# Attention softmax in a two-layer DiT kernel: the multiplication by the reciprocal sum moves from VectorE to GpSimd

## What is computed

```python
def _attend(q, k, v):
    s = jnp.einsum('bqhgd,bkhd->bhgqk', q * HEAD_DIM ** -0.5, k).astype(jnp.float32)
    p = jax.nn.softmax(s, axis=-1).astype(v.dtype)
    return jnp.einsum('bhgqk,bkhd->bqhgd', p, v)
```

## Time and profile before

| | us |
|---|---|
| Median of 3 runs | 3375.95 |
| Profiled execution, its time | 3370.39 |
| Profiled execution, its span in the trace | 3368.6 |
| Pairs of layer 0 (24 pairs), from 1106.90 to 1200.40 | 93.50 |
| Pairs of layer 1 (16 pairs), from 2898.60 to 2959.90 | 61.30 |
| PE busy over the span | 3188.0 |
| DVE busy over the span | 1731.9 |
| ACT busy over the span | 1409.3 |

### The profile page before, as it was taken

The page is one execution under the profiler, slowest core; times in us unless marked ns, Lnnn a source line. Parts: engine busy times, 40 slices in busy tenths (PEclk is TensorE's granted clock), DMA queues, the critical chain, the costliest instruction groups (busy, mean ns, idle before and its releaser), DMA issues.

```text
span 3368.6 us, 51444 instructions
## 1 busy us (share of the span) xinstructions
PE 3188.0 (95%) x18766; PEld 2650.5 (79%) x18766; DVE 1731.9 (51%) x3150; ACT 1409.3 (42%) x2197; POOL 131.5 (4%) x126
## 2 busy tenths in 40 slices
PE   4999999999989899999999999999899998899898
PEld 2777768888868578877788868787788888699898
DVE  2333357777743833434333343333678775756555
ACT  3222255565534632224322242223655654653544
POOL 0000001010100000000000000000000000000000
PEclk7999999999999999999999999999899999999999
DMA  6534431111122033222432243444211113144454
GB/s 234 175 127 151 153 113 45 50 50 44 54 66 88 14 115 130 99 87 95 168 100 94 94 144 137 162 133 153 73 48 51 61 45 115 60 142 164 152 183 146
DMA packets 101116, 363.43 MB, mean 108 GB/s; under 512 B 11136, under 2 KB 12672, under 8 KB 100864
## 3 DMA queue, kind: packets, MB, share of 16 engines
q1 hardware_dynamic: 98240, 353.02, 31.0%
q10 hardware_dynamic: 2752, 8.72, 0.8%
HBM read 360.58 MB, written 1.11 MB: 107 GB/s over the span
## 4 chain that ended last, share of the span: by engine, by line
PE 84%; DVE 7%; ACT 4%; issue 3%; DMA 1%; POOL 0%; SPq 0%; DVEq 0%; POOLq 0%; ACTq 0%
PE bank L1598 67%; PE bank L1847 3%; PE bank L1845 2%; DVE wlo L989 2%; PE bank L1623 2%; ACT whi L480 1%; PE bank L1898 1%; ACT scr L910 1%; PE bank L1906 1%; DVE h L1056 1%; PE bank L1916 1%; PE bank L1918 1%; PE bank L2051 1%; PE bank L2074 1%; ACT gc_row L893 1%
## 5 line engine op out<-in xcount | busy, mean ns | idle before, releaser
L1598 PE MATMUL bank<-uh,whi 128*128 128x512 f32 (+1 forms) x3008 | 1117.2, 371 | 49.6 <-ACTq L868 17.0
L1598 PE MATMUL bank<-ul,whi 128*128 128x512 f32 (+1 forms) x3008 | 1084.3, 360 | 0.0
L1598 PE MATMUL bank<-uh,wlo 128*128 128x512 f32 (+1 forms) x3008 | 1081.8, 360 | 0.5 <-DVE scr L1346 0.3
L480 ACT ACTIVATE whi<-raw 128x1024 fp32r<-128x1024 f32 x520 | 548.1, 1055 | 1223.1 <-PE bank L1598 1222.7
L989 DVE TENSOR_TENSOR wlo<-raw,whi 128x1024 fp32r<-128x1024 f32 x520 | 642.0, 1235 | 799.1 <-ACT whi L480 797.7
L1598 PEld LDWEIGHTS bank<-uh,whi 128*128 128x128 f32 x3008 | 577.7, 192 | 155.9 <-issue 60.4
L1598 PEld LDWEIGHTS bank<-uh,wlo 128*128 128x128 f32 x3008 | 576.7, 192 | 82.0 <-DVE scr L1346 1.8
L1598 PEld LDWEIGHTS bank<-ul,whi 128*128 128x128 f32 x3008 | 578.4, 192 | 69.9 <-issue 2.2
L1598 PE MATMUL bank<-bh,whi 128*128 128x512 f32 (+1 forms) x1088 | 387.9, 357 | 1.1 <-DVE h L1056 0.8
L1598 PE MATMUL bank<-bl,whi 128*128 128x512 f32 (+1 forms) x1088 | 384.5, 353 | 0.0
L1598 PE MATMUL bank<-bh,wlo 128*128 128x512 f32 (+1 forms) x1088 | 384.4, 353 | 0.0
(11 more groups left out here) (232 smaller groups left out, 3034.3 us busy)
## 6 DMA issues: line engine op xcount, KB each, us to landing
raw<-stream SPq DMA_DIRECT2D x520, 512.0 KB, 3.3
ada_raw<-stream SPq DMA_DIRECT2D x132, 512.0 KB, 5.1
gc_row<-gc_rows ACTq DMA_DIRECT2D x16, 512.0 KB, 3.7
m<-stream SPq DMA_DIRECT2D x8, 512.0 KB, 11.4
scr<-stream SPq DMA_DIRECT2D x4, 512.0 KB, 13.0
h<-h_in SPq DMA_DIRECT2D x1, 2048.0 KB, 17.3
cst<-consts SPq DMA_DIRECT2D x1, 1298.0 KB, 5.6
out<-m SPq DMA_DIRECT2D x8, 128.0 KB, 1.8
```

What stands on the lines that cost most here:

```text
L480: act.activation(whi[:, j, :], raw[:, j, :], ACT.Copy).then_inc(hi_ready, 1)
L1598: last = mm(bank[j][:, c0:T], w(t, a), x[:, t, c0:T], start=n == 0, stop=n == 3 * kts - 1)
```

## The change

VectorE computes the reciprocal alone and signals a new semaphore `s_recip`. A new function `shares(l)` in GpSimd's program waits for it and does the multiplications in place, in the same order and the same shapes, and signals `s_scaled`, on which TensorE's transposes wait as before. On GpSimd it stands between the delta-rule heads and the squares of the layer's last norm.

```diff
             "s_sum", "s_max", "s_exp", "s_recip", "s_scaled", ...
+            def shares(l):
+                n0 = att_pairs_before(l)
+                for n, (j, kind) in enumerate(att_pairs(l)):
+                    w = 1 if kind else 2
+                    for a in range(2):
+                        st = 16 * (n % 2) + 8 * a
+                        pool.wait_ge(A["s_recip"], 2 * (n0 + n) + a + 1)
+                        for q in range(w):
+                            k = 512 // w
+                            pq = Pb[:, n % 2, a, q * k:(q + 1) * k]
+                            last = pool.tensor_scalar(pq, pq, stat[:, st + 6 + q:st + 7 + q], None, ALU.mult)
+                        last.then_inc(A["s_scaled"], 1)
+
             for l in range(DEPTH):
                 squares(3 * l)
                 squares(3 * l + 1)
                 heads(l)
+                shares(l)
                 squares(3 * l + 2)
...
                         dve.wait_ge(A["s_exp"], 2 * (n0 + n) + a + 1)
-                        steps.do(dve.reciprocal(stat[:, st + 6:st + 6 + w], stat[:, st + 4:st + 4 + w]))
-                        steps.sync()
-                        for q in range(w):
-                            k = 512 // w
-                            pq = Pb[:, n % 2, a, q * k:(q + 1) * k]
-                            last = dve.tensor_scalar(pq, pq, stat[:, st + 6 + q:st + 7 + q], None, ALU.mult)
-                        last.then_inc(A["s_scaled"], 1)
+                        dve.reciprocal(stat[:, st + 6:st + 6 + w], stat[:, st + 4:st + 4 + w]).then_inc(A["s_recip"], 1)
                     out_low(n - 3)
```

More of the change, by code:

```diff
@@ L270, in build @@
             "a_x", "a_sq", "a_sum", "a_var", "a_rstd", "a_norm", "a_swap", "a_done", "a_vx", "a_vturn", "a_vtok",
-            "s_sum", "s_max", "s_exp", "s_scaled", "s_turned", "s_pt", "s_pv", "att_hi", "att_low")}
+            "s_sum", "s_max", "s_exp", "s_recip", "s_scaled", "s_turned", "s_pt", "s_pv", "att_hi", "att_low")}
         C = {n: sem(n) for n in ("c_vec", "c_p4", "c_out", "c_hi", "c_ready", "br_gate", "mh_ready", "mx_ready")}
```

## The result

The changed kernel takes 3381.74 us (median of 10 runs, 3376.81 to 3383.69). The kernel before took 3373.43 in 10 runs shared with it (3370.50 to 3377.99). The ratio is 1.0022, with a 95% interval of 1.0012 to 1.0031: 8.3 us slower. The forecast was 3.8 us faster and no difference that could be told. The time lies inside the range of 3366 to 3388, but the change went the other way.

What follows compares the result with a forecast made beforehand. It took a loop between TensorE, VectorE and ScalarE to bound the pairs, VectorE's queue limiting at layer 0's tile boundaries. Gains 3.0 + 0.5 + 0.3 = 3.8 us off the median 3375.95 gave 3372, range 3366 to 3388.

Steps and rivals of the forecast that it cites:

- VectorE's relief: Pairs of both layers: time won by taking 96 multiplications off VectorE's queue, 3.8 us, at most 4.1.
- 3.0 + 0.5 + 0.3 = 3.8 us: Gain: six tile boundaries of layer 0 at 0.5 each, layer 1's start 0.5, layer 0's start 0.3.
- The boundary between tiles: Layer 0, every three pairs: the next maximum starts 0.50 us earlier without the multiplication, period 10.3 instead of 10.79.
- The value of D: Time of one GpSimd multiplication of 512 columns: taken as 1.1 us, with ends of 0.49 and 1.73.
- The stated end of 1.73: Upper end for a 512-column GpSimd multiplication, from its product when VectorE works beside it with several SBUF operands.
- The slack: Time before TensorE's turn waits for GpSimd: up to 1.46 us per multiplication in layer 1, 0.76 for kind 0's 256 columns.
- 2D + 3.8: Length in us of the loop of two pairs through GpSimd, D one multiplication's time; it is 6.71 at D = 1.46.
- The start: First pair of each layer: gain 0.5 us in layer 1, 0.1 to 0.5 in layer 0, where some tenths may go.
- GpSimd becomes the bound: Rival: the turn waits for `s_scaled` from D = 1.46; +9 us at 1.73, about +25 at 2.0; chance 0.16.
- The rival of the shared access: VectorE's small operations wait for GpSimd at their common access to SBUF: +20 us, 3396; chance 0.08.
- The 0.6 us over 40 pairs: Shared SBUF access: mean wait of the negation at D = 1.29, 24 us before subtracting the gain.
- More than forecast: Rival: VectorE's shorter queue also shortens the chain's maxima in each pair, gain over 6.7 us; chance 0.08.

Runs made afterwards that it cites:

- e1: Changed kernel with no engine multiplying by the reciprocal, transposes waiting for the reciprocal: 3371.82 against 3372.56 us for the kernel before, ratio 0.9997.
- e4: Changed kernel with a constant 1/256 in place of the reciprocal operand on GpSimd: 1.488 and 0.848 us per multiplication, periods 10.49 and 6.71 us.
- e3: Changed kernel with GpSimd's multiplication written as tensor_tensor, the reciprocal broadcast as second input: 3373.91 us, ratio 1.0002 to the kernel before.
- e2: Changed kernel with only half the columns of each multiplication done on GpSimd, hand-overs kept: 3373.15 us in one run.
- e5: Changed kernel with the first pair of each layer multiplied by VectorE, the others on GpSimd: 3379.10 us in one run.
- e6: Changed kernel with kind 0's two-column negation written as two one-column instructions: 3383.47 us in one run.
- e7: Kernel before with six of 96 multiplications moved to GpSimd, layer 0, second head of kind 3: 3372.66 against 3373.07 us, ratio 0.9995.
- e9: Kernel before with six multiplications on GpSimd and kind 0's negation split into two one-column instructions: 3372.01 against 3372.09 us, ratio 0.9998.
- e8: Changed kernel with broadcast tensor_tensor multiplications on GpSimd and each layer's first pair on VectorE: 3369.13 against 3373.07 us for the kernel before, ratio 0.9985.

## Why the prediction was wrong, point by point

**What bounds the kernel, and VectorE's relief: right.** The sum was 3.0 + 0.5 + 0.3 = 3.8 us, at most 4.1. Its upper end, with 0.5 for layer 0's start too, adds up to 4.0, not 4.1. Without a multiplication e1 has 3.83 in layer 0 and 0.49 in layer 1, periods of 10.26 and 6.71. The boundary between tiles gave 0.53 for each period.

**The value of D: this step failed.** It says "I take something below it, 1.1", because a multiplication by one number reads one tile and the product reads two. The multiplication measured 1.565 us for 512 columns and 0.925 for 256. The inference from fewer inputs to less time was false: the operation has 2.5 ns for each column (e4) and the two-input product 1.7 when its second input is a broadcast (e3). The stated end of 1.73 held it. With 1.565 the slack of 1.46 is overrun, and TensorE's turns wait for GpSimd. The Trainium skill, "GPSIMD Engine Reference", has one-input work at roughly line rate ("4.1 Engine selection") and, as the best case of a loop over 512 elements, 769 ns ("3.1 Elementwise"). This case's rows have 1565 ns and, with a constant, 1488; the measurement decides.

**The slack: right.** "D up to 1.46": layer 1 loses nothing at 1.488 (e4) and 0.17 us of 6.71 at 1.565. The formula 2D + 3.8 gives 6.93 there, and 6.88 was measured. For kind 0 the slack was 0.76 us for 256 columns, and 0.925 overran it, which is what the chain of layer 0 shows. "Up to D = 1.29 nothing waits in the rhythm" holds in e2 and e3.

**The start: a second term that failed.** It stood with some tenths in layer 0 and with nothing in layer 1. The rival took only the loss of its gain. It cost 3.3 + 1.8 us, more than the rhythm's 2.0 + 1.2. By the chain only some 0.6 us of layer 0's part are the wait for GpSimd. The rest is that TensorE's clock, already up, falls back to its lower level for the next scores, pv and turn, which nothing in the prediction had; e5 shows that both go together. Even at 1.04 us (e3) the start cost 0.7 + 0.8 us.

**The rival "GpSimd becomes the bound" happened**, at 0.16 where the forecast had 0.68. Its +9 us for D = 1.73 is near the 8.3 measured, though made up otherwise: the rhythm is less than it had, and the start more. So the nearness is luck. That 3381.74 lies in the range is owed to this rival, for which the range was stretched to 3388, and not to the forecast of 3372.

**The rival of the shared access is there, and small.** Only kind 0's two-column negation waits, 0.09 us on average (263 ns against the 168 to 171 of the kernel before), 0.17 in each period's chain (e6: 0.12 for each period, under 1 us in all). The 0.6 us over 40 pairs didn't come: one column never waits. The Trainium skill, "SBUF — State Buffer", section "Who interferes with whom", has a `tensor_scalar` in the two-port mode wait for the whole instruction of GpSimd. The Trainium skill, "VectorE: DVE Perf Modes", section "Mode 2×_2P", has the condition: an outermost non-unit dimension that is even, or odd and equal for source and destination. The trace agrees as far as two columns wait and one doesn't, and in e7 the wait ends with the instruction of GpSimd, 1155.20 against 1155.18. In the changed kernel itself 12 of the 16 two-column negations take longer than 171 ns. Six of them, of 254 ns, end with GpSimd's instruction; the other six, of 330 to 338 ns, end in the middle of one, which I can't explain from the rows.

**"More than forecast": nothing of it.** Layer 1's periods are the same to 0.01 us in all kernels with short multiplications.

**The unit of the sum.** I took a gain in the chain of the pairs for a gain in the total. The medians show that of 4.3 us only 0.7 arrives in e1, none of 2.3 in e9, and all of 3.1 in e8. At this size the rest of the kernel isn't a constant: TensorE's clock at later restarts moves by as much as the gain.

## What to carry to other kernels

Before moving an elementwise operation to GpSimd, work out the slack of its consumer and measure that very form of instruction there: the number of its inputs says nothing of its time, and the slack decides at once between a small gain and a loss. Leave the first items of a pipeline, which nothing hides, on the fast engine, above all where TensorE waits for them and its clock falls. A gain of a tenth of a percent in one stage has to be confirmed in the whole time, with enough runs; the trace of the stage alone can overstate it.

## What the runs showed of the hardware

- GpSimd, float32, 128 partitions: `tensor_scalar` with a scalar per partition 1565, 925 and 602 ns for 512, 256 and 128 columns; with a constant 77 ns less; `tensor_tensor` of two tiles 1289 and 733; `tensor_tensor` with a broadcast second input 1039 and 612. The slowest form is the one with the fewest data.
- VectorE beside GpSimd: a `tensor_scalar` inside SBUF with two columns waits (up to 395 ns in e7, 570 in e5, against 171 with GpSimd idle), one with one column doesn't (152 ns in e6), a maximum from PSUM doesn't (0.69 us in e7).
- TensorE: after a wait at the same place of the program, the granted clock over the next 10 us differed from kernel to kernel: 1.00 or 0.84 behind the pairs of layer 0, worth 1.46 us, and 0.84 or 0.72 in front of the third branch, worth 1.1 us. The two kernels that ran twice repeated theirs.
- TensorE: its clock, back at 1.00 since 1111, fell to 0.50 at the start of layer 0 after it had worked 0.66 of 3.2 us, and the next pieces took up to 0.9 us longer each.
